# Expert loops of a mixture-of-experts block: the narrow block ahead of the wide one in every trip

## The reference

```python
affinity = sigmoid(h @ router_w)
_, idx = top_k(affinity + router_bias, TOP_K)              # 6 experts per token
gates = s_sel / sum(s_sel) * ROUTED_SCALE
def expert_block(acc, blk):                                # tokens of one expert
    tok, g, e = blk
    y = swiglu(h_ext[tok], w_gate[e], w_up[e], w_down[e])  # (silu(x@wg) * (x@wu)) @ wd
    return acc.at[tok].add(y * g[:, None]), None
out = acc[:n_tok] + swiglu(h, ws_gate, ws_up, ws_down)
```

## Time and profile before

| | us |
|---|---|
| median of 3 runs | 2565.54 |
| lowest and highest run | 2559.32, 2566.08 |
| the profiled execution: its own time | 2561.44 |
| its span, first to last instruction | 2559.7 |
| layer 0: 34 trips with both kinds | about 710 to 1412 |
| layer 0: 4 narrow blocks alone | about 1412 to 1450 |
| layer 1: 16 trips with both kinds | about 1899 to 2222 |
| layer 1: 34 narrow blocks alone | about 2222 to 2527 |

### The profile page before, as it was taken

How to read it: one execution, slowest core, us unless ns; L and a number is a source line. 1 busy time by engine, 2 the same in 40 slices (tenths; PEclk the granted TensorE clock), 3 DMA queues, 4 the chain that set the end, 5 groups by cost and what they waited for, 6 DMA issues and landing times. The chain is left out here.

```text
span 2559.7 us, 39554 instructions
## 1 busy us (share of the span) xinstructions
PE 2148.3 (84%) x11733; PEld 1190.5 (47%) x11734; DVE 908.9 (36%) x2012; ACT 607.8 (24%) x1047; POOL 453.5 (18%) x423
## 2 busy tenths in 40 slices
PE   5889999896999999999999516489789999987873
PEld 3665445644444444444444315154444444444442
DVE  8854375824512121111111267922431111111113
ACT  3443243602122121121212113130222122211110
POOL 1000000002112222222222211200113222232321
PEclk8999999998999999999999858799899999999997
DMA  9971102005699999999998557960389999899995
GB/s 354 374 266 38 36 30 82 1 0 194 263 334 359 352 358 359 354 358 350 356 364 286 178 181 245 272 224 0 144 353 380 353 358 358 277 388 365 392 379 196
DMA packets 167668, 672.72 MB, mean 263 GB/s; under 512 B 37858, under 2 KB 40898, under 8 KB 123546
## 3 DMA queue, kind: packets, MB, share of 16 engines
q1 hardware_dynamic: 116650, 577.23, 58.8%
q0 software_dynamic: 38208, 69.04, 11.1%
q10 hardware_dynamic: 12720, 25.27, 2.6%
HBM read 622.28 MB, written 89.24 MB: 278 GB/s over the span
## 5 line engine op out<-in xcount | busy, mean ns | idle before, releaser
L1431 PE MATMUL banks_l<-slotw_l,xTw_l 128*128 128x512 f32 x800 | 357.9, 600 | 24.8 <-issue 24.8
L1442 PE MATMUL banks_l<-slotn_l,xTn_l 128*64 128x256 f32 x2816 | 326.5, 385 | 35.1 <-issue 35.1
L1442 PEld LDWEIGHTS banks_l<-slotn_l,xTn_l 128*64 128x64 f32 x2816 | 212.1, 138 | 180.9 <-issue 107.8
L1431 PEld LDWEIGHTS banks_l<-slotw_l,xTw_l 128*128 128x128 f32 x800 | 148.5, 191 | 236.1 <-issue 236.1
L1481 PE MATMUL banks_l<-slotn_l,late_l 128*64 128x512 f32 x704 | 189.9, 615 | 18.2 <-DVE late_l L1283 16.3
L1460 PE MATMUL banks_l<-slotw_l,late_l 128*128 128x512 f32 x400 | 191.8, 602 | 15.4 <-DVE late_l L1269 15.4
L946 POOL DMA_INDIRECT xgw_l<-moe_h,idxw_l x58 | 60.7, 1047 | 770.9 <-PE banks_l L1376 634.5
L974 POOL DMA_INDIRECT moe_acc<-late_l,idxn_l x88 | 141.1, 1603 | 200.8 <-DMA moe_acc<-late_l,idxn_l 183.4
L1266 DVE TENSOR_TENSOR late_l<-late_l,banks_l 128x256 f32<-128x256 f32 x50 | 21.1, 422 | 341.0 <-ACT late_l L1072 341.0
L1231 DVE TENSOR_TENSOR onehotn_l<-iota_slot_l,rank_l 128x512 bf16 (+1 forms) x98 | 79.3, 809 | 133.5 <-issue 133.5
L556 PE MATMUL ps_a<-W_a,hT_a 128*128 128x512 f32 x288 | 124.1, 592 | 0.0
(11 more groups left out here) (397 smaller groups left out, 3057.0 us busy)
## 6 DMA issues: line engine op xcount, KB each, us to landing
slotn_l<-in_exp_w_gate SPq DMA_DIRECT2D x88, 1024.0 KB
slotn_l<-in_exp_w_up SPq DMA_DIRECT2D x88, 1024.0 KB
slotn_l<-in_exp_w_down SPq DMA_DIRECT2D x88, 1024.0 KB
slotw_l<-in_exp_w_gate SPq DMA_DIRECT2D x50, 1024.0 KB
slotw_l<-in_exp_w_up SPq DMA_DIRECT2D x50, 1024.0 KB
slotw_l<-in_exp_w_down SPq DMA_DIRECT2D x50, 1024.0 KB
w_p<-in_mod_w SPq DMA_DIRECT2D x12, 2048.0 KB, 15.7
ZU_s<-in_mod_w SPq DMA_DIRECT2D x8, 2048.0 KB, 16.4
```

The source lines that it names most:

```text
L1431: last = pe.matmul(pGU_w, xT_w[b % 2][:, k, :], wgu[0][b % WIDE_RING][:, :, k, :], start=(k == 0), stop=(k == KD - 1))
L1442: last = pe.matmul(pGU_n[H * side:H * side + H, b % 2], xT_n[b % 2][:, k % 4, H * (k // 4):H * (k // 4) + H], w[:, :, k, P * side:P * side ...
```

## The change

In every trip the narrow block's step now stands ahead of the wide block's, on all engines and in the weight loads. On DVE two functions are cut differently besides: the copy of the narrow transposed hidden block moves from `rest_narrow` to `gated_narrow`, and the copy of the wide one from `gated_wide` to `rest_wide`. Nothing is added or taken away, and what is loaded before the first trip keeps its order.

```diff
-            trips(sp, count(sp, 0), count(sp, 1), (next_gate_up(0), next_gate_up(1), next_down(0), next_down(1)))
+            trips(sp, count(sp, 0), count(sp, 1), (next_gate_up(1), next_gate_up(0), next_down(1), next_down(0)))
...
-            trips(pool, nw, nn, ((0, wide, 0), (1, narrow, 0)))
+            trips(pool, nw, nn, ((1, narrow, 0), (0, wide, 0)))
...
-                  ((0, silu_wide, 0), (1, silu_narrow, 0), (0, rest_wide, 0), (1, rest_narrow, 0)))
+                  ((1, silu_narrow, 0), (0, silu_wide, 0), (1, rest_narrow, 0), (0, rest_wide, 0)))
...
             def gated_wide(i, q, b):
                 dve.wait_ge(W['silu_done'], i + 1)
                 dve.tensor_tensor(hid_w, hsil_w, pGU_w[:, 1, :], ALU.mult).then_inc(W['hid_done'], 1)
+
+            def gated_narrow(i, q, b):
+                dve.wait_ge(N['silu_done'], i + 1)
+                dve.tensor_tensor(hid_n, hsil_n, pGU_n[:, b % 2, 1, :], ALU.mult).then_inc(N['hid_done'], 1)
+                dve.wait_ge(N['hidT_mm'], i + 1)
+                dve.wait_ge(N['y_mm'], i + NARROW_RING)
+                dve.tensor_copy(hidT_n, pHT[:, 0, :]).then_inc(N['hidT_done'], 1)
+
+            def rest_wide(i, q, b):
                 dve.wait_ge(W['hidT_mm'], i + 1)
                 dve.wait_ge(W['y_mm'], i + WIDE_RING)
                 dve.tensor_copy(hidT_w, pHT).then_inc(W['hidT_done'], 1)
-
-            def gated_narrow(i, q, b):
-                dve.wait_ge(N['silu_done'], i + 1)
-                dve.tensor_tensor(hid_n, hsil_n, pGU_n[:, b % 2, 1, :], ALU.mult).then_inc(N['hid_done'], 1)
-
-            def rest_wide(i, q, b):
                 dve.wait_ge(yw_added, i * 16 + 16)
                 tokens(0, i + AHEAD, (b + AHEAD) % UNROLL)
                 mark_wide(i + (AHEAD + 1))
 
             def rest_narrow(i, q, b):
-                dve.wait_ge(N['hidT_mm'], i + 1)
-                dve.wait_ge(N['y_mm'], i + NARROW_RING)
-                dve.tensor_copy(hidT_n, pHT[:, 0, :]).then_inc(N['hidT_done'], 1)
                 dve.wait_ge(yn_added[b % 2], q * (16 * UNROLL // 2) + 16 * (b // 2) + 16)
...
-                  ((0, gated_wide, 0), (1, gated_narrow, 0), (0, rest_wide, 0), (1, rest_narrow, 0)))
+                  ((1, gated_narrow, 0), (0, gated_wide, 0), (1, rest_narrow, 0), (0, rest_wide, 0)))
...
-            trips(pe, n_wide, n_narrow, ((0, up_wide, 0), (1, up_narrow, 0), (0, rest_wide, 0), (1, rest_narrow, 0)))
+            trips(pe, n_wide, n_narrow, ((1, up_narrow, 0), (0, up_wide, 0), (1, rest_narrow, 0), (0, rest_wide, 0)))
```

## The result

The changed kernel takes 2588.87 us (median of 6 runs, 2581.14 to 2595.84), the kernel before 2560.03 us beside it (6 runs, 2556.91 to 2566.08): a ratio of 1.0104, 95% interval 1.0086 to 1.0122. That is 28.8 us or 1.0% slower; the forecast was 2588 us. The profiled execution of the changed kernel took 2581.14 us, its span is 2579.4 us. PE's busy time in it is the same, 2148.7 us against 2148.3.

A forecast was written before the change was run, and what follows sets the result against it. PE was taken to bound the both-kind trips, with DMA close behind. Terms 29.9 + 9.0 - 8.5 - 3.6 - 2.0 = +24.8 us on 2561.44 gave 2586.2, or 2590.3 by the median; forecast 2588 us, 8-in-10 range 2571 to 2606.

The forecast's parts named there:

- Term 4: Change to narrow blocks alone, both layers: the second add may come earlier; -2 us, bounds 0 and -5.
- PE sets the pace: Both-kind trips go at PE's pace; idle time moved or made there counts in full, unless the loads take over.
- Term 1: Wide down-product waits for DVE's wide copy behind the narrow one-hot: +29.9 us in layer 0, +9.0 in layer 1.
- Term 2: Narrow hidden copy no longer behind the wide one-hot, so PE's narrow down-product waits less: -8.5 us in layer 0, layer 1 nothing.
- Term 3: First product's extra wait at every sixth trip should vanish: 7 turns of 0.52 us, -3.6 us.
- the loads set the pace: Rival: loads release both-kind trips, so new PE idle time is hidden; time within 3 us of 2561.4 to 2565.5; chance 0.09.
- the DMA share would fall to 0.94: Sign in the changed kernel's timeline: DMA share about 0.94, from 0.96 to 0.97 while both kinds run.
- register reads run ahead: Rival: DVE's reads before the narrow one-hot finish during its wait for the pick; -14 us, about 2549; chance 0.04.
- The branches between one-hot and copy: Two DVE branches, given no cost; if behind the one-hot, 0.25 us a trip, sum 12 us larger.
- late wide weights: Rival: wide loads, now behind narrow, late by 1 us a trip: 50 us more, about 2638; chance 0.09 for all above 2605.
- The slower restart of PE after the longer gap: Named as an example of smaller costs between forecast and slower rival, unsized; within the 0.09 chance for all above 2605.

The follow-up runs named there:

- again: The changed kernel timed and profiled once more, nothing altered: 2586.89 us, ratio 1.0089 to the kernel before.
- 7: One extra DVE sum (768 or 512 elements) behind each narrow one-hot: on the changed kernel 2678.42 us, on the kernel before 2564.54 us.
- 8: The changed kernel with a shorter extra DVE sum (256 elements, 0.41 us) behind each narrow one-hot: 2633.91 us, ratio 1.0278 to the kernel before.
- 1: The changed kernel with DVE's wide hidden copy put ahead of the narrow one-hot and its register reads: 2538.56 us, ratio 0.9912 to the kernel before.
- 4: The kernel before with PE's wait for the narrow index moved behind both up-products of the next trip: 2537.51 us, ratio 0.9907.
- experiment 5: The kernel before with PE's narrow-index wait behind the next trip's up-products and DVE's narrow hidden copy ahead of the wide one-hot: 2525.32 us, ratio 0.9852.
- experiment 3: The kernel before, old order, with DVE's narrow hidden copy put ahead of the wide one-hot: 2560.75 us, ratio 0.9992.
- 6: The changed kernel with DVE's wide hidden copy ahead of the narrow one-hot and PE's narrow-index wait moved later: 2529.02 us, ratio 0.986 to the kernel before.

## Why the prediction was right, point by point

| stage, us in the profiled execution | before | predicted | changed | again | loads in old order |
|---|---|---|---|---|---|
| layer 0, 34 trips with both kinds | 701.8 | +18.8 | 718.9 | 717.4 | 717.5 |
| layer 0, narrow alone | 39.5 | -1 | 38.1 | 39.8 | 39.9 |
| between the loops (not changed) | 447.5 | 0 | 443.3 | 451.9 | 452.0 |
| layer 1, 16 trips with both kinds | 322.8 | +8.0 | 330.8 | 330.4 | 330.4 |
| layer 1, narrow alone | 305.0 | -1 | 306.4 | 305.4 | 305.2 |

The prediction for layer 0 is +29.9 - 8.5 - 2.6 (5 turns), for layer 1 +9.0 - 1.0 (2 turns); Term 4 is halved between the layers here.

- **PE sets the pace:** right for the change and for every slower kernel. PE's idle time that was put in (7, 8) came back in the time in full or more, and what was taken away (1, 4, 5) came back in the trips; only in experiment 3 PE's own next wait took it. But the loads' own pace was close behind: at trips of 20 us they fall behind, and in the new order PE at last waits for them (experiments 5 and 6).
- **Term 1, the new wait,** was sized at 2.95 us from the index to the wide down-product. In the timeline above it is 1042.90 - 1039.98 = 2.92. Against 2.07 before it is 0.85 in place of 0.88, +28.9 us in layer 0. How the wait divides was off by a bit: I had 0.36 us of idle time before the wide transpose and 1.2 before the down-product, and it is hardly any and 1.45. The transpose starts 0.49 us after the index (1061.64 - 1061.15), not 0.78. The sum hangs on the end of DVE's chain alone, and did not notice.
- **Term 2, the narrow copy,** was sized at -8.5 us: 13.9 us of waits became 3.9, -10.0. Right.
- **Term 3, the loop's turn:** right; trips at a turn are 21.14 to 21.20 us in layer 0 of the changed kernel, its others (but for the one of 22.74) 20.93 to 21.23, while before they were mostly 21.08 against 20.61. In layer 1 something is left of it: 20.96 and 20.72 at its two turns, against 20.59.
- **Term 4, narrow blocks alone,** -2 us: not to be seen. The three runs in the new order give -1.4, +0.3 and +0.4 in layer 0 and +1.4, +0.4 and +0.2 in layer 1. The first add may leave earlier; the stage does not end earlier.
- Trips with both kinds together took 25.1, 23.2 and 23.3 us more, against a forecast of +26.8. The medians differ by 28.8 and 26.1 us. The part between the loops, which the change does not touch, is 443 to 455 us long from one profile to another, so single executions can't be compared closer than that; its 443.3 in the first profile is why that pair differs by 19.7 us only. What is left between the trips' 23 to 25 us and the medians' 26 to 29 is within this scatter, and stays open.
- **The rival "the loads set the pace"** falls for this change: PE's new idle time came in full on top. Faster trips were to be had too (19.88 us) with more bytes a second, though not for long (experiment 5). My forecast that the DMA share would fall to 0.94 failed too: it stayed at 0.97 with 340 GB/s, where it was 350. The share hardly follows the traffic, and its value before left some 5% that it did not show. The rule that I had set beside it, to take the engine of highest occupancy first (the Trainium skill, Perfetto Trace Analysis, Identifying the Most-Contended Engine), would have pointed to DMA; its own warning, that occupancy misleads for DMA, fits this trace, whose share was 0.99 at 354 and at 348 GB/s (experiment 5).
- **The rival "register reads run ahead"** falls: 47.3 / 34 = 1.39 us before the one-hot, as before. The branches between one-hot and copy cost nothing: the copy starts at 1042.25, 0.08 us before the one-hot's end at 1042.33. The 51 and 108 ns of the Trainium skill (Advanced Engine Details and Errata, Control Flow Timing) are hidden here. My estimate from them was also added up wrongly: the two make 0.16 us a trip and not 0.25, or 8 us in all and not 12.
- **The rival "late wide weights"** falls at trips of 21 us: with the loads in their old order the time is the same, and no wait of PE in the expert loops of the changed kernel names a load of weights. At trips of 20 us in the new order it came true in a small way (experiments 1 and 6: 3.1 and 6.1 us in the profiled executions). The slower restart of PE after the longer gap, which I had named in half a sentence as a smaller cost, does exist, but at 1.45 us it happened once in 102 trips.

## What to carry to other kernels

When two jobs alternate on several engines and share buffers, price a swap not by the order of the jobs but by what then stands, on the helper engine, between PE's result and the copy that PE waits for; here one operation and its register reads were worth 50 us, and which job comes first made no difference to the usual trip. Look next for waits that stand earlier than their resource is needed: a wait moved behind 11 us of other products gave 0.9%, and only then did the better order of copies on DVE show its own gain. Before a saving ahead of such a wait is counted, follow it through that wait (experiment 3). And when trips get shorter, read the time from issue to landing of the loads early and late in the loop: if it grows, the loads are the next limit, long before a wait on one is seen.

## What the hardware showed beyond what was expected

- Idle time of PE can cost more than itself. With a gap before the wide down-product in each trip, PE busy for 7.1 + 3.7 us of up-products and more between, the granted clock fell for the products behind the gap in about half the trips at 1.8 us and in most at 2.3 us, and 1.15 us was lost on the first four matmuls alone (3.11 us for 1.96). At 1.45 us it fell once in the layer 0 of three profiles, at 0.5 us or less at none of the places looked at. These are gaps of this loop, and no rule was looked for. By trips, 2.31 us of gap cost 23.55 - 21.15 = 2.4 us more than 1.44 us did, where the gap alone is 0.87 longer.
- The reads of two numbers from a table into registers take DVE 1.28 to 1.47 us in the median ahead of a one-hot of 0.96 us, in every kernel and order of these runs. They were the larger part of the wait that the change made.
- The share of the DMA engines was 0.99 both at 354 and at 348 GB/s, and 1.00 at 371. It counts transfers under way, and in this kernel it did not tell 0 from 5% left. What told it was the time from a load's issue to its landing, which stood still at trips of 21.15 us (7.7 and 9.3 us) and grew at trips of 19.88 us (12.5 to 28.9 us).
